# Adding expert results by an accumulating indirect transfer to device memory instead of by TensorE and VectorE

## The reference, cut to what matters

```python
logits = jnp.dot(t, w_router)                       # t: 256 x 1024
top_logit, top_idx = lax.top_k(logits, 2)
gate = jax.nn.softmax(top_logit, axis=-1)
...
def expert_block(args):                             # rows of one expert
    x_blk, e = args
    return (jax.nn.silu(x_blk @ w1[e]) * (x_blk @ w3[e])) @ w2[e]
...
y = jnp.zeros_like(t).at[slot_tok].add(yb * slot_gate[:, None])
x = x + y                                           # then the final RMSNorm
```

## Time and profile before

| | |
|---|---|
| runs | 1459.90, 1460.94, 1468.07 us; median 1460.94 |
| profiled execution, span from first to last instruction | 1459.0 us (its time outside the span is not listed) |
| median of the runs less that span | 1.9 us |
| TensorE busy | 1395.9 us, 96% |
| VectorE, ScalarE, GpSimd busy | 1129.3, 893.5, 350.5 us |
| expert layer | from about 660 us to the end |
| bytes moved by DMA | 378.85 MB, mean 260 GB/s |

### The profile page before, as it was taken

The page is one execution under the profiler, slowest core; times in us unless marked ns, Lnnn a source line. Parts: engine busy times, 40 slices in busy tenths (PEclk is TensorE's granted clock), DMA queues, the critical chain, the costliest instruction groups (busy, mean ns, idle before and its releaser), DMA issues.

```text
span 1459.0 us, 23545 instructions
## 1 busy us (share of the span) xinstructions
PE 1395.9 (96%) x8569; PEld 1141.5 (78%) x8569; DVE 1129.3 (77%) x1036; ACT 893.5 (61%) x913; POOL 350.5 (24%) x428
## 2 busy tenths in 40 slices
PE   5989999999999999999999999999999999999997
PEld 4778777788877787777888888878888888788885
DVE  6967667655555577677889889898888898988886
ACT  4445555544345455555777777777777777777775
POOL 3888715998000187000000000000000000000000
PEclk9999999999999999998999999999999999999998
DMA  9433354565655332685999999999999999999981
GB/s 243 144 104 116 120 170 145 188 200 176 198 177 165 107 117 88 247 310 207 368 370 355 357 370 352 354 371 348 368 357 358 369 350 364 362 349 335 388 292 29
DMA packets 193075, 378.85 MB, mean 260 GB/s; under 512 B 17777, under 2 KB 57073, under 8 KB 192882
## 3 DMA queue, kind: packets, MB, share of 16 engines
q1 hardware_dynamic: 188256, 367.51, 71.8%
q0 software_dynamic: 2608, 7.87, 2.0%
q10 hardware_dynamic: 2146, 2.59, 0.6%
HBM read 374.78 MB, written 2.10 MB: 258 GB/s over the span
## 4 chain that ended last, share of the span: by engine, by line
PE 82%; DVE 7%; ACT 5%; issue 2%; DMA 1%; POOL 1%; SPq 0%; ACTq 0%; POOLq 0%; DVEq 0%
PE bank L641 79%; DVE lo L1568 4%; ACT hi L1175 3%; PE bank L1063 1%; PE bank L659 1%; DMA raw<-in_ssm_c_im_dram 1%; DMA raw<-in_w_in_dram 1%; ACT at_hi L1494 1%; POOL raw L2185 1%; POOL raw L2129 0%; PE bank L1044 0%; DVE raw L1678 0%; DVE bank L1680 0%; PE bank L967 0%; ACT at_hi L1478 0%
## 5 line engine op out<-in xcount | busy, mean ns | idle before, releaser
L1568 DVE TENSOR_TENSOR lo<-raw,hi 128x2048 fp32r<-128x2048 f32 x347 | 802.7, 2325 | 174.0 <-ACT hi L1175 173.8
L1175 ACT ACTIVATE hi<-raw 128x2048 fp32r<-128x2048 f32 x347 | 662.9, 1916 | 192.7 <-PE bank L641 191.7
L641 PE MATMUL bank<-hi,at_hi 128*128 128x512 f32 x1280 | 511.7, 400 | 16.1 <-DVE lo L1568 5.4
L641 PE MATMUL bank<-hi,at_lo 128*128 128x512 f32 x1280 | 500.9, 391 | 0.0
L641 PE MATMUL bank<-lo,at_hi 128*128 128x512 f32 x1280 | 499.9, 391 | 0.0
L641 PEld LDWEIGHTS bank<-hi,at_hi 128*128 128x128 f32 x1280 | 241.4, 189 | 71.1 <-DVE lo L1568 13.9
L641 PEld LDWEIGHTS bank<-hi,at_lo 128*128 128x128 f32 x1280 | 240.9, 188 | 52.2
L641 PEld LDWEIGHTS bank<-lo,at_hi 128*128 128x128 f32 x1280 | 241.6, 189 | 47.0
L641 PE MATMUL bank<-hi,ht_hi 128*128 128x512 f32 x440 | 172.1, 391 | 7.3 <-DVE lo L1568 4.7
L2232 POOL DMA_INDIRECT qk<-xn_rows,slot_row x7 | 18.7, 2670 | 651.9 <-DVE slot_row L2079 473.7
L641 PE MATMUL bank<-hi,ht_lo 128*128 128x512 f32 x440 | 171.4, 389 | 0.0
(11 more groups left out here) (285 smaller groups left out, 1149.6 us busy)
## 6 DMA issues: line engine op xcount, KB each, us to landing
raw<-in_moe_w_dram SPq DMA_DIRECT2D x528, 512.0 KB, 5.6
raw<-in_ffn_w_dram SPq DMA_DIRECT2D x66, 512.0 KB, 4.3
raw<-in_w_in_dram SPq DMA_DIRECT2D x64, 512.0 KB, 4.6
raw<-in_w_branch_dram SPq DMA_DIRECT2D x16, 512.0 KB, 4.1
raw<-in_w_out_dram SPq DMA_DIRECT2D x16, 512.0 KB, 6.5
raw<-in_w_glu_dram SPq DMA_DIRECT2D x4, 512.0 KB, 4.3
xres<-in_x_dram SPq DMA_DIRECT2D x2, 512.0 KB, 6.2
raw<-in_ssm_c_re_dram POOLq DMA_DIRECT2D x4, 256.0 KB, 6.5
```

The source lines that it names most:

```text
L641: return pe.matmul(o, a, b, start=start, stop=stop)
L1175: act.activation(hi[:, slot, :], src, ACT.Copy).then_inc(hi_ready, 1)
L1568: tt(lo[:, slot, :], src, hi[:, slot, :].bitcast(f32), SUB).then_inc(lo_ready, 1)
```

## The change

For every block but the last, the results no longer go through `combine` and `add_block`.

- Before the loop GpSimd copies `xres` to `moe_sum`, a tensor in device memory of 256 rows and 128 spare rows, in three transfers of 512 KB.
- `place_numbers` takes the place of `place_t`: two matmuls with 3 columns give the gate, the token number and a 1 for each slot. On VectorE `numbers_of` writes `place_gate` and `token_row` (empty slots get a spare row each), in step 2; it waits until the block before has been added (`y_out`).
- ScalarE writes the result times the gate as float32 into `y_rows` (in `ureg`), and signals `ye_ready` itself. VectorE's `result_lo` goes.
- GpSimd adds the 128 rows to `moe_sum` by one accumulating indirect transfer, behind a small instruction that passes the wait (`after`).
- After the last turn GpSimd loads `moe_sum` back into `xres`, and VectorE waits for that before it adds the last block.

```diff
             def hidden_t(b, c):
                 pe.wait_ge(h_done, b * NEC + (2 * NCH + c + 1))
-                if c == 1:
-                    pe.wait_ge(x_added, b * 4 + 9)
...
-            def combine(b):
-                pe.wait_ge(gt_ready, b + 1)
-                pe.wait_ge(ye_ready, b + 1)
-                for i, bank in enumerate(comb_banks):
-                    n, th = i // 2, i % 2
-                    mm(bank[:, :], gate_t[:, th, :], at_hi[:, 4 * n:4 * n + 4, P:2 * P], True, False)
-                    mm(bank[:, :], gate_t[:, th, :], at_lo[:, 4 * n:4 * n + 4, P:2 * P], False, True).then_inc(comb_full, 1)
+            def place_numbers(b):
+                for th in range(TH):
+                    m = mm(TR[1][:, 0:3], place[:, th, :], numbers[:, :, th], th == 0, th == 1)
+                m.then_inc(pg_full, 1)
...
-            def result_hi(b, used):
+            def result(b, used):
                 act.wait_ge(tile_used, used)
+                act.wait_ge(gt_ready, b + 1)
                 for n in range(2):
-                    m = act.activation(at_hi[:, 4 * n:4 * n + 4, P:2 * P], PY[n][:, :].rearrange("p (k c) -> p k c", k=4),
-                                       ACT.Copy, scale=place_gate)
-                m.then_inc(ye_hi_ready, 1)
+                    m = act.activation(y_rows[:, n * 512:(n + 1) * 512], PY[n][:, :], ACT.Copy, scale=place_gate)
+                m.then_inc(ye_ready, 1)
...
+            ts(numbers[:, 1, :], cst[:, C_ROW:C_ROW + TH], -1.0, float(SEQ), MUL, ADD)
+            dve.memset(numbers[:, 2, :], 1.0)
             dve.wait_ge(logits_full, 1)
...
-            def result_lo(b):
-                dve.wait_ge(ye_hi_ready, b + 1)
-                for n in range(2):
-                    m = stt(at_lo[:, 4 * n:4 * n + 4, P:2 * P], ...)
-                m.then_inc(ye_ready, 1)
-            def add_block(b):
-                for i, bank in enumerate(comb_banks):
-                    ...
-                    dve.wait_ge(comb_full, b * 4 + (i + 1))
-                    tt(z, z, bank[:, :], ADD).then_inc(x_added, 1)
+            def numbers_of(b):
+                dve.wait_ge(pg_full, b + 1)
+                dve.wait_ge(y_out, b * 16 + Y_START)
+                dve.tensor_copy(place_gate, TR[1][:, 0:1])
+                own.step(stt(row_tmp, TR[1][:, 2:3], 0.0, cst[:, C_SLOT:C_SLOT + 1], ALU.is_equal, MUL))
+                tt(token_row[:, :], TR[1][:, 1:2], row_tmp, ADD).then_inc(gt_ready, 1)
...
                 if c == 2 and not final:
-                    dve.wait_ge(gt_ready, b + 1)
+                    numbers_of(b)
                     own.step(dve.tensor_copy(column, ...))
                     places().then_inc(place_ready, 1)
...
+            pool.wait_ge(x_added, 12)
+            for i, th in enumerate((0, 1, 0)):
+                pool.dma_start(moe_sum[i * P:(i + 1) * P, :], xres[:, th, :]).then_inc(y_out, 16)
             pool.wait_ge(routed, 1)
...
+            def rows_added():
+                pool.indirect_dma_start(moe_sum[:, :], bass.IndirectOffsetOnAxis(ap=token_row[:, 0:1], axis=0), y_rows, None,
+                                        compute_op=ADD).then_inc(y_out, 16)
+            def after(i):
+                tt(small[:, 82 + i:83 + i], ident[:, 0:1], ident[:, 0:1], MUL).then_inc(pool_passed, 1)
             pool.wait_ge(rows_out, 16 * (TH + 1))
             pool.wait_ge(slot_ready, 1)
+            rows_in_order()
+            pool.wait_ge(y_out, Y_START)
             with pool.Fori(0, last - 1) as b:
+                pool.wait_ge(ye_ready, b + 1)
+                after(0)
+                rows_added()
+                pool.wait_ge(slot_ready, b + 2)
+                after(1)
                 rows_in_order()
-                pool.wait_ge(slot_ready, b + 2)
-            rows_in_order()
+                pool.wait_ge(y_out, b * 16 + (Y_START + 16))
+                pool.wait_ge(pool_passed, b * 2 + 2)
+            pool.wait_ge(ye_ready, last)
+            after(2)
+            rows_added()
+            pool.wait_ge(y_out, last * 16 + Y_START)
+            after(3)
+            for th in range(TH):
+                pool.dma_start(xres[:, th, :], moe_sum[th * P:(th + 1) * P, :]).then_inc(back_in, 16)
```

More of the change, by code:

```diff
@@ L43 @@
 C_ID, C_TRI, C_ONE, C_IOTA, C_SEL, C_COS, C_SIN = 0, 128, 256, 384, 512, 640, 768
-C_ROW, C_END = 896, 898
+C_ROW, C_SLOT, C_END = 896, 898, 899
 GROUPS = (0, 2, 1, 3)
@@ L160, in build @@
         half_scores = sem("half_scores")
-        table = sb("table", [P, 5], i32)
+        table = sb("table", [P, 6], i32)
         slot_row = sb("slot_row", [P, 1], i32)
+        token_row = table[:, 5:6]
+        moe_sum = nc.dram_tensor("moe_sum", (SEQ + P, D), f32, kind="Internal").ap()
+        y_out, back_in = sem("y_out"), sem("back_in")
+        pool_passed = sem("pool_passed")
         xn_rows = nc.dram_tensor("xn_rows", (SEQ + 1, D), f32, kind="Internal").ap()
@@ L405, in build @@
         place_gate = small[:, 93:94]
+        numbers = small[:, 74:80].rearrange("p (k t) -> p k t", t=TH)
+        row_tmp = small[:, 80:81]
+        y_rows = u_flat
+        Y_START = 16 * 3
         comb_banks = (TR[0], TR[1], PV[0], PV[1])
@@ L1101, in last_combine @@
                         mm(bank[:, :], gate_t[:, th, :], at_lo[:, 4 * n:4 * n + 4, P:2 * P], False, True).then_inc(tail_comb, 1)
-            def combine(b):
-                pe.wait_ge(gt_ready, b + 1)
-                pe.wait_ge(ye_ready, b + 1)
-                for i, bank in enumerate(comb_banks):
-                    n, th = i // 2, i % 2
-                    mm(bank[:, :], gate_t[:, th, :], at_hi[:, 4 * n:4 * n + 4, P:2 * P], True, False)
-                    mm(bank[:, :], gate_t[:, th, :], at_lo[:, 4 * n:4 * n + 4, P:2 * P], False, True).then_inc(comb_full, 1)
+            def place_numbers(b):
+                for th in range(TH):
+                    m = mm(TR[1][:, 0:3], place[:, th, :], numbers[:, :, th], th == 0, th == 1)
+                m.then_inc(pg_full, 1)
             def place_t(b):
-                pe.wait_ge(x_added, b * 4 + 12)
                 for th in range(TH):
@@ L1128, in expert_step @@
                         down(b, c, at, kind)
-                        if c == NEC and kind == "w2a":
-                            combine(b)
                     elif not (final and chunk == NEC):
@@ L1147, in expert_step @@
                 if c == 1:
-                    place_t(b)
+                    if final:
+                        place_t(b)
+                    else:
+                        place_numbers(b)
             pe.wait_ge(place_ready, 1)
@@ L1505, in expert_step @@
                     split_to(b, at + 2, final)
-                if c == 2:
+                if c == 2 and final:
                     act.wait_ge(pg_full, b + 1)
@@ L1513, in expert_step @@
                 if c == NEC:
-                    result_hi(b, b * FFN_TILES + (T_MOE + place_in_step(c - 1, "w2") + 1))
+                    result(b, b * FFN_TILES + (T_MOE + place_in_step(c - 1, "w2") + 1))
                 split_to(b, at + 3, final)
@@ L2027, in _ @@
             own.step(ts(r_tab[:, 0:1], r_rank[:, NE - 1:NE], float(NE - 1), None, ADD))
-            dve.tensor_copy(table[:, :], r_tab).then_inc(routed, 1)
+            dve.tensor_copy(table[:, 0:5], r_tab).then_inc(routed, 1)
             gathered(1)
@@ L2041, in hidden_lo_of @@
                    ht_rows_hi[:, 0:h_width(c) // P, :].bitcast(f32), SUB).then_inc(ht_lo_ready, 1)
-            def result_lo(b):
-                dve.wait_ge(ye_hi_ready, b + 1)
-                for n in range(2):
-                    m = stt(at_lo[:, 4 * n:4 * n + 4, P:2 * P], PY[n][:, :].rearrange("p (k c) -> p k c", k=4), place_gate,
-                            at_hi[:, 4 * n:4 * n + 4, P:2 * P].bitcast(f32), MUL, SUB)
-                m.then_inc(ye_ready, 1)
-            def add_block(b):
-                for i, bank in enumerate(comb_banks):
-                    n, th = i // 2, i % 2
-                    z = xres[:, th, n * 512:(n + 1) * 512]
-                    dve.wait_ge(comb_full, b * 4 + (i + 1))
-                    tt(z, z, bank[:, :], ADD).then_inc(x_added, 1)
+            def numbers_of(b):
[4 more added lines that the diff above has]
+                tt(token_row[:, :], TR[1][:, 1:2], row_tmp, ADD).then_inc(gt_ready, 1)
             def split_to(b, at, final):
@@ L2067, in expert_step @@
                 hidden_lo_of(b, c)
-                if c == NEC:
-                    result_lo(b)
                 if final and c == NEC - 1:
@@ L2085, in expert_step @@
                     split_to(b, i, final)
-                    if c == NEC and i == at + 5:
-                        add_block(b)
             for j in range(2, 6):
@@ L2094, in _ @@
             with dve.Fori(0, last) as b:
-                own.loop(b, 1)
+                own.loop(b, 2)
                 for c in range(1, NEC + 1):
@@ L2104, in _ @@
```

(2 more changed lines are left out.)

## The result

| | before | after |
|---|---|---|
| median of the runs | 1465.08 us (seven runs, with the three shown first) | 1448.91 us (seven runs) |
| ratio of the runs, 95% interval | | 0.9902, 0.9880 to 0.9923 |
| span of the profiled execution | 1459.0 us | 1452.4 us (its own time 1454.24) |
| a turn of the expert loop, from one gather to the next, mean of six | 97.70 us | 95.70 us |

The ratio says that 14.4 us of 1465.08 are gone (11.3 to 17.6); the two medians lie 16.2 us apart, inside that interval. The forecast was 12.95 less, reckoned from the 1460.94 of the first three runs. That its absolute 1448.0 lies only 0.9 us from the measured 1448.91 is partly luck: over seven runs the kernel before is 4.1 us slower than over the first three.

A forecast was written before the change was run, and what follows sets the result against it. TensorE was taken to bound the kernel. -14.5 (TensorE) + 1.3 (`numbers_of`) + 0.25 (router) = -12.95 us, so 1460.94 becomes 1448.0 us, chance 0.70; own range 1442 to 1451, extended to 1457 for rivals.

The forecast's parts named there:

- The bound: Expert loop: TensorE, busy 96.94 of 97.75 us a turn, is the bound; the queues' 361 GB/s is what it asks for.
- TensorE's part: Seven loop turns: the combine's matmuls, 1.85 us, and place_t's two transposes, 0.22 us, leave each turn; 14.5 us in all.
- VectorE's relief at 0: Expert loop: VectorE's four additions and result_lo go, but lie beside matmuls, so 0; w2b meets no new wait.
- `numbers_of`: Step 2: three added one-column VectorE operations take 0.45 us, of which 0.2 a turn shows, 1.3 us in all; bounds 0 and 2.5.
- The stall: TensorE's 0.7 us wait before w2a, behind result copies, hi and lo, stays: 0; if gone, 4.7 us more.
- The add's wait: VectorE's wait for y_out in numbers_of: 40 us available, the add's landing has lower bound 9.4, so 0.
- The router's stage: Two new VectorE operations ahead of the router's logits cost 0.25 us, once.
- (a): Rival: gather or a hand-over comes late, up to 5.3 us over seven turns, 1453 us; chance 0.12.
- (b): Rival: queues are full at 360 GB/s in a long stream, only 3 us won, 1458 us; chance 0.09.
- (c): Rival: the accumulating transfer holds the engines; slower than before from 9.7 us, 1477 us at 12; chance 0.09.

The follow-up runs named there:

- experiment 1: Changed kernel with eight 128 x 512 matmuls put back between w2a and w2b of step 6: turn 97.50 us, ratio to the kernel before 0.9983.
- experiment 4: Changed kernel with the accumulating add transfer taken away: turn 95.67 us, ratio 0.9920; with it issued three times in sequence: 95.70 us, 0.9896.
- experiment 3: Kernel before with VectorE's difference and additions alone removed: turn 97.72 us, ratio 1.0013; with the eight combine matmuls alone removed: 96.66 us, 0.9947.
- experiment 6: Changed kernel with ScalarE's two result copies put behind its hi for w2a: turns 95.10 and 95.09 us, medians 1443.37 and 1442.78 us.
- first kernel of experiment 6: First of two executions of the changed kernel with ScalarE's hi ahead of the result copies: turn 95.10 us, ratio to the kernel before 0.9872.
- experiment 7's second kernel: Kernel before with wait, one-column GpSimd operation and gather following each other without a loop branch between: turn 97.66 us, one run.
- experiment 7's first kernel: Kernel before with a one-column GpSimd operation ahead of each loop gather, the loop branch in between: turn 97.70 us, one run.

## Why the prediction was right

**The bound.** TensorE, not the queues: shown by experiments 1 and 4. 361 GB/s in the loop was demand, and the room above it is to 390.

**TensorE's part.** 7 x (1.85 + 0.22) = 14.5 forecast. The matmuls measured 1.80 in experiment 1; with the transposes' 0.22, which no run took alone, that is 2.02.

**VectorE's relief at 0.** Right in the sum, incomplete in the reason that I gave it. By itself the relief is worth 0 (experiment 3). But the prediction looked only at whether `w2b` would meet a late `lo`; the wait would come at the fourth tile from `w2a`, the first whose `lo` stands behind the four additions. Had the additions stayed, some 0.8 us of the matmuls' 1.85 would have been given back. They left with the matmuls, so the 1.85 counts in full: the number was right without the step that it needed.

**`numbers_of`.** 0.2 us a turn forecast, with bounds 0 and 0.35; about 0.1 measured. Its operations take 0.37 instead of 0.45 (919.75 to 920.12), and TensorE starts the next tile at 923.12, 12 x 0.227 behind the start of the one before at 920.40, without a wait. That tile then lasts 2.83 us (to 925.95), where the same one in the kernel before lasts 2.72 (822.34 to 825.06). Over seven turns the term was taken 0.5 us too large, half of the 1 us by which the forecast was too small. Timeline of step 2 in the kernel after, beside the earlier trace rows:

```profile
919.75 0.15 DVE L2052 COPY small<-bank 128x1 f32<-128x1 f32 x1
...
920.12 0.17 DVE L2072 COPY small<-gates 128x4 f32 x1
...
920.73 4.49 DVE L1571 TENSOR_TENSOR lo<-raw,hi 128x2048 fp32r<-128x2048 f32 x2
...
923.12 0.45 PE L649 MATMUL bank<-hi,ht_hi 128*128 128x512 f32 x1
```

**The stall.** Forecast to stay, stayed, and for the chain that the prediction named: experiment 6 took the copies out of it and the stall was gone.

**The add's wait.** It lands after 8.7 to 9.8 us, near the lower bound of 9.4, under the 40.

**The router's stage.** 0.25 forecast, none measured. The first of the two new operations stands in the chain with 0.08 us, but the operation behind it has become shorter there by as much: from the start of the last pair on `qk` to the second operation on `gates` it is 1.56 us before (653.65 to 655.21) and 1.53 after (660.46 to 661.99).

**The rivals.** (a) fell: the gather lands sooner, not later. In part that is luck, since the 2 us that it saves on GpSimd were not foreseen; with them added back it would land after 8.8 to 9.8 us, an estimate from the rows above, and still inside the 8.4 to 10.2 of before. (b) fell: 390 GB/s. The Trainium skill's 358 GB/s for a core (DMA: Bandwidth & Descriptors, Specifications) is not the ceiling of this run, in which one core is at work; its HBM Reference (Specifications (TRN2)) says that a core streaming alone measures well above its share, and these traces agree, with 390. (c) fell: the add holds the engines 2.5 us.

**Together.** 7 x 2.0 = 14.0 us less by the turn, 13.8 from the first `place_t` to the last, 14.4 by the runs, 12.95 forecast. The 1 us between forecast and measured is mostly `numbers_of` and the router's stage. Term by term the turn gives 2.02 - 0.1 = 1.9 of the measured 2.00; 0.1 us a turn isn't accounted for.

## What to carry to other kernels

Work that "lies beside" other work is worth nothing alone, but ask what covers it: matmuls and additions that hide each other are worth more together than the sum of the two, and either alone disappoints. When weights stream near the queues' limit, reckon in two numbers, the rate that the queues give and the time in hand by which tiles are early; extra bytes cost nothing until the second is spent. After such a change look again for the stall that remains: here the order of two steps on ScalarE was worth another 4 us.

## What the runs showed of the hardware that was not expected

- **GpSimd is held by VectorE's `lo`.** The `lo` is a tensor_tensor of 128 x 2048 with both inputs in SBUF, 2.29 us. In all traces, a gather that starts 0.08 to 0.33 us behind its start takes 2.83 to 3.03 us on GpSimd; one that starts ahead of it, or at most 0.04 us behind its start (the last gather before, at 1325.45 beside a `lo` at 1325.44), takes 0.94 to 1.04. The accumulating transfer is held in the same way: in experiment 4 those that start 0.19 to 0.25 us behind a `lo` take 3.48 to 3.54 us, the others 1.54 to 1.65. So is the small operation: 1.14 us instead of 0.19 in the first kernel of experiment 6. The Trainium skill (SBUF — State Buffer, Who interferes with whom) says that such a VectorE instruction contends with a GpSimd instruction that reads SBUF; the rows agree, if the transfer reads its row numbers there, which no run here separates. The same section reports that a tensor_tensor did not stall a transfer issued by GpSimd; for these indirect ones the rows show that it does.
- **A wait right on a transfer costs GpSimd more than one on a small operation.** From the end of `slot_row` to the gather's start it is 0.84 us where the gather stands right behind the wait (the first gather of experiment 7's second kernel, 741.20 to 742.04) and 0.42 with the small operation between (1034.37 to 1034.79). With the loop's branch behind the wait it is 0.99 in the kernel before (1129.14 to 1130.13), and 1.10 in experiment 7's first kernel (1134.80 to 1135.90), where the small operation gains nothing.
- **The accumulating transfer is cheap.** 128 rows of 4 KB added in device memory: 1.59 us on GpSimd, 9.0 to landing, 2.5 us of the sixteen engines (2.6 each by experiment 4, (9.2% - 1.5%) of 100 us for three).
